# Computing the first 512 features behind each norm token tile by token tile, on a one-core transformer kernel

## The reference

```
h = rmsnorm(x, g);      x = x + short_conv_mixer(h)      # norm 0 before
x = x + conv_ffn(rmsnorm(x, g))                          # norm 1 before
x = x + moba_attention(rmsnorm(x, g))                    # norm 2 before
x = x + conv_ffn(rmsnorm(x, g));  x = rmsnorm(x, g)      # norm 3 before, norm 4 behind
x = layer_norm(ALPHA * x + even_mixer(x), g, b)          # norm 5
x = layer_norm(ALPHA * x + swiglu(x), g, b)              # norm 6
x = layer_norm(ALPHA * x + odd_mixer(x), g, b)           # norm 7
x = layer_norm(ALPHA * x + swiglu(x), g, b)              # norm 8, the output
```

## Time and profile before

| | us |
|---|---|
| median of 3 runs | 1309.02 (1308.71 to 1309.11) |
| the profiled execution | 1310.29 |
| its span, first to last instruction | 1309.0 |
| TensorE busy (matmul) | 1264.8 (97%) |
| VectorE busy | 815.9 (62%) |
| ScalarE busy | 616.7 (47%) |
| GpSimd busy | 68.7 (5%) |
| weights read | 211 MB in the span, 44% of the DMA engines' time |

### The profile page before, as it was taken

How to read it: one execution, slowest core, us unless ns; L and a number is a source line. 1 busy time by engine, 2 the same in 40 slices (tenths; PEclk the granted TensorE clock), 3 DMA queues, 4 the chain that set the end, 5 groups by cost and what they waited for, 6 DMA issues and landing times.

```text
span 1309.0 us, 20175 instructions
## 1 busy us (share of the span) xinstructions
PE 1264.8 (97%) x8548; PEld 1163.8 (89%) x8548; DVE 815.9 (62%) x1087; ACT 616.7 (47%) x775; POOL 68.7 (5%) x94
## 2 busy tenths in 40 slices
PE   7999999999998999999999999999998899999997
PEld 7999999887877999988998789999888887999986
DVE  6656777647665777763786675554467466655544
ACT  6445555434554555543674434443335653544430
POOL 0000000001000000000225200000001000000000
PEclk9999999999999999999999999999999999999999
DMA  9554454554431345554443345445434322644530
GB/s 356 213 194 154 185 194 172 213 190 182 161 129 65 145 181 176 192 194 176 169 161 131 132 186 190 172 184 199 169 121 161 130 97 97 225 173 182 193 129 32
DMA packets 32857, 219.37 MB, mean 168 GB/s; under 512 B 4224, under 2 KB 4480, under 8 KB 7680
## 3 DMA queue, kind: packets, MB, share of 16 engines
q1 hardware_dynamic: 30896, 211.27, 44.3%
q0 software_dynamic: 1872, 6.82, 1.5%
HBM read 217.01 MB, written 1.05 MB: 167 GB/s over the span
## 4 chain that ended last, share of the span: by engine, by line
PE 89%; DVE 6%; ACT 3%; issue 1%; POOL 1%; DMA 0%; DVEq 0%; ACTq 0%; POOLq 0%
PE ps L756 33%; PE ps L729 16%; PE ps L733 16%; PE ps L730 16%; PE ps L769 1%; DVE t L1272 1%; PE ps L791 1%; PE ps L818 1%; ACT t L991 1%; DVE t L1319 1%; POOL t L1634 1%; DMA t<-in_rows 0%; PE ps L803 0%; ACT t L1041 0%; PE ps L819 0%
## 5 line engine op out<-in xcount | busy, mean ns | idle before, releaser
L1272 DVE TENSOR_TENSOR t<-t,t 128x2048 fp32r<-128x2048 f32 (+2 forms) x201 | 454.9, 2268 | 173.5 <-PE ps L756 132.5
L756 PE MATMUL ps<-t,t 128*128 128x512 f32 (+2 forms) x2088 | 491.1, 392 | 12.3 <-DVE t L1341 3.6
L756 PEld LDWEIGHTS ps<-t,t 128*128 128x128 f32 x2088 | 384.5, 189 | 91.8 <-issue 9.5
L991 ACT CAST t<-t 128x2048 fp32r<-128x2048 f32 (+1 forms) x199 | 376.5, 1895 | 167.1 <-PE ps L756 151.3
L729 PE MATMUL ps<-t,t 128*128 128x256 f32 x1808 | 454.9, 284 | 0.2
L730 PE MATMUL ps<-t,t 128*128 128x256 f32 x1808 | 453.3, 283 | 0.0
L729 PEld LDWEIGHTS ps<-t,t 128*128 128x128 f32 x1808 | 347.0, 192 | 1.3 <-issue 1.0
L730 PEld LDWEIGHTS ps<-t,t 128*128 128x128 f32 x1808 | 347.0, 192 | 0.1
L733 PE MATMUL ps<-t,t 128*128 128x256 f32 x1808 | 290.6, 283 | 0.0
L733 PEld LDWEIGHTS ps<-t,t 128*128 128x128 f32 x1808 | 249.5, 192 | 0.0
L1329 DVE SCALAR_TENSOR_TENSOR t<-ps,t,t 128x255 f32<-128x255 f32 (+2 forms) x212 | 87.3, 476 | 51.3 <-ACT t L1006 42.1
(11 more groups left out here) (188 smaller groups left out, 743.9 us busy)
## 6 DMA issues: line engine op xcount, KB each, us to landing
t<-in_wts SPq DMA_DIRECT2D x196, 1024.0 KB, 4.8
t<-in_rows POOLq DMA_DIRECT2D x13, 512.0 KB, 4.6
t<-in_wts SPq DMA_DIRECT2D x2, 768.0 KB, 4.1
t<-in_x_in SPq DMA_DIRECT2D x2, 512.0 KB, 3.8
t<-in_wts SPq DMA_DIRECT2D x2, 512.0 KB, 3.6
out<-t SPq DMA_DIRECT2D x4, 256.0 KB, 2.0
t<-in_cst SPq DMA_DIRECT2D x1, 448.0 KB, 10.9
t<-in_pw SPq DMA_DIRECT2D x1, 256.0 KB, 5.8
```

The source lines that it names most:

```text
L756: ins = mm(ps[:, t_bank(stage, t, j), 0:c1 - c0], a, w[:, k, c0:c1], start=kt == 0 and part == 0, stop=kt == KTS[stage] - 1 and part == 2)
L991: copy(wh[:, k, 0:w], wraw[:, r, 0:w]).then_inc(s_hi, 1)
L1272: tt(wl[:, k, sl], wraw[:, r, sl], wh[:, h, sl].bitcast(F32), ALU.subtract).then_inc(s_lo, 1)
```

## The change

Behind norms 1 to 7 the first 512 features are computed as a **head**: in form T with one accumulator per token tile, tile 0 first. `head_steps` writes the order: all high passes of tile 0 (8 contraction tiles x 2 matmuls), then its low passes with the turning of tile 1's two halves among them, then tile 1. For the FFNs and the even mixer's u, the next stages want features by tokens; ScalarE copies each tile's result from PSUM to SBUF ("evict", into XN's tile 0) and TensorE turns it into banks 2 and 3 ("headturn"), from which what read chunks 0 and 1 now reads. q0 and cq are used as they lie. The head of an FFN holds 256 gate and 256 up features; its weights are packed as two chunks of four contraction tiles.

The warming matmuls behind the norms go (those at the program's start stay). At a layer norm the centring is a step of its own, and tile 0's two "rest" steps lie between tile 1's centrings and scalings. In an FFN the convolutions, silu and product of chunks 0 and 1 come after chunk 2, together with chunk 2's. In the even mixer the order becomes: u (the head), dt, x parts; dtsoft stands behind xconv0, and "ends" behind the second x chunk. In the odd mixer the fourth pump of the head stands before lrms0, where it stood behind it.

```diff
     def ffn(q, up_g, up_u, g0, u0, down, layer):
-        for m in range(11):
+        head(f"ffn{q}", (up_g, up_u), layer, [(g0, 256), (u0, 256)])
+        for m in range(1, 11):
...
+    head("even", ("even_w_in_2",), 0, [(0, 512)])
     f("even", "even_w_in_2", 0, 3072, 16, 128)
-    for m in range(2):
-        f("even", "even_w_in_2", 0, 256 * m)
...
-@q0 t0.0 t1.0 t2.0 t3.0 t4.0 t5.0 flush + t6.0 t7.0 t0.1 t1.1 t2.1 t3.1 t4.1 t5.1 t6.1 t7.1 + +
+@q0 head
...
-f0.0 dtcopy + f1.0 dtin f1.1 us0 + dtsoft f2.0 sum0 f2.1 us1 +
-f3.0 f3.1 xconv0 + xsilu0 mix0 f4.0 f4.1 sum1 xconv1 + xsilu1 ends f5.0 f5.1 xconv2 + xsilu2
-mix1 f6.0 f6.1 sum2 xconv3 + xsilu3 btok cb f7.0 mix2 f7.1 sum3 xconv4 + xsilu4 spread0
-f8.0 f8.1 xconv5 + xsilu5 mix3
+@even head f0.0 headturn dtcopy us0 us1 + f1.0 dtin sum0 f1.1 xconv0 + dtsoft xsilu0 sum1
+f2.0 mix0 f2.1 xconv1 + xsilu1 ends f3.0 mix1 f3.1 sum2 xconv2 + xsilu2 f4.0 f4.1 sum3 xconv3 + xsilu3 mix2
+f5.0 btok cb f5.1 xconv4 + xsilu4 spread0 mix3 f6.0 f6.1 xconv5 + xsilu5
...
-@cq t0.0 t0.1 t1.0 t1.1 t2.0 t2.1 t3.0 t3.1 + t4.0 t4.1 t5.0 t5.1 t6.0 t6.1 t7.0 t7.1 lrms0 +
+@cq head lrms0
...
-    elif b < 5:
-        out += [("warm", b, 6, WARM_RMS[0]), ("rest", b, 0, 0), ("stats", b, 1), ("rest", b, 0, 1),
-                ("norm", b, 1, 0), ("turn", b, 1, 0), ("warm", b, 7, WARM_RMS[1]), ("norm", b, 1, 1),
-                ("turn", b, 1, 1), ("rest", b, 1, 0), ("rest", b, 1, 1)]
-    else:
-        out += [("warm", b, 6, WARM_LN[0]), ("stats", b, 1), ("norm", b, 1, 0), ("turn", b, 1, 0),
-                ("warm", b, 7, WARM_LN[1]), ("norm", b, 1, 1), ("turn", b, 1, 1),
-                ("rest", b, 0, 0), ("rest", b, 1, 0), ("rest", b, 0, 1), ("rest", b, 1, 1)]
-    return out + [("pump",)] * (1 if lazy else 2)
...
+    if b < 5:
+        return out + [("rest", b, 0, 0), ("stats", b, 1), ("rest", b, 0, 1), ("norm", b, 1, 0), ("norm", b, 1, 1)]
+    return out + [("stats", b, 1), ("centre", b, 1, 0), ("rest", b, 0, 0), ("norm", b, 1, 0), ("rest", b, 0, 1),
+                  ("centre", b, 1, 1), ("norm", b, 1, 1)]
...
+def head_steps(h, b):
+
+
+    stage = f"head_{h}" if h in HEADED else h
+    lo = [("lo", stage, kt, 0) for kt in range(8)]
+    n = 4 if b >= 5 else 0
+    out = [("hi", stage, kt, 0) for kt in range(8)] + lo[:n] + [("turn", b, 1, 0)]
+    n, m = n, (8 if b >= 5 else 2)
+    out += lo[n:m] + [("turn", b, 1, 1)] + lo[m:]
+    if h in HEADED:
+        out.append(("evict", h, 0))
+    out += [("rest", b, 1, 0), ("rest", b, 1, 1), ("pump",), ("pump",)]
+    out += [("t", stage, kt, 1) for kt in range(4)] + [("pump",)]
+    if h in HEADED:
+        out.append(("headturn", h, 0))
+    out += [("t", stage, kt, 1) for kt in range(4, 8)]
+    if h in HEADED:
+        out.append(("evict", h, 1))
+    return out + [("pump",)]
+
+
+def ffn_steps(q, b):
+    out = head_steps(f"ffn{q}", b - 1)
+    for n in range(2, 22):
+        out += [("f", f"ffn{q}", n, 0)] + [("headturn", f"ffn{q}", 1)] * (n == 2) + [("f", f"ffn{q}", n, 1)]
+        done = (0, 1, 2) if n == 2 else (n,)
+        for m in done:
+            name = "product" if m % 2 else "silu"
+            out += [("conv", q, m)] * (q < 2) + [("pump",)] * (m == n) + [(name, q, m // 2)]
...
+        def head_turned(stage, t):
+            pe.wait_ge(*head_copied(stage, t))
+            for i in range(4):
+                if i % 2 == 0:
+                    pe.wait_ge(*acc_free(f_ready(stage), 1, i // 2))
+                ins = turn(head_bank(t, i), head_rows(t)[:, tok(i)], ident)
+            ins.then_inc(s_headt, 1)
...
+            elif kind == "evict":
+                stage, t = k
+                act.wait_ge(s_t, T_AT[("lo", f"head_{stage}", 7, 0) if t == 0 else ("t", f"head_{stage}", 7, 1)])
+                act.wait_ge(s_turn, xh_at(f_ready(stage), 0, t))
+                copy(head_rows(t), ps[:, t, :]).then_inc(s_headc, 1)
```

More of the change, by code:

```diff
@@ L31, in t, with head @@
             plan.append((stage, "T", name, layer, [(c0, n)], n, per, k))
+    def head(stage, name, layer, cols):
+        for k in (0, 4):
+            plan.append((f"head_{stage}", "T", name, layer, cols, 512, 4, k))
     def ffn(q, up_g, up_u, g0, u0, down, layer):
-        for m in range(11):
+        head(f"ffn{q}", (up_g, up_u), layer, [(g0, 256), (u0, 256)])
+        for m in range(1, 11):
             f(f"ffn{q}", up_g, layer, g0 + 256 * m)
@@ L80, with f_chunk @@
 KTS = {stage: len(c) * PER[stage] for stage, c in CHUNKS.items()}
+HEADED = ("ffn0", "ffn1", "ffn2", "ffn3", "even")
+def f_chunk(stage, n):
+    return CHUNKS[stage][n - 2 if stage[:3] == "ffn" else n]
 VEC = {}
@@ L185, in mixed_steps @@
             steps.append(("pump",))
-        elif word == "flush":
-            steps += [("turn", 2, 1, 0), ("turn", 2, 1, 1), ("rest", 2, 1, 0), ("rest", 2, 1, 1)]
+        elif word == "head":
+            steps += head_steps(stage, b - 1)
+        elif word == "headturn":
+            steps.append(("headturn", stage, 1))
         elif word == "end":
@@ L227, in end_steps @@
-    return out + [("pump",)] * (1 if lazy else 2)
-def ffn_steps(q, b, lazy=False):
-    out = []
-    for n in range(22):
-        out += [("f", f"ffn{q}", n, 0), ("f", f"ffn{q}", n, 1)]
-        name = "product" if n % 2 else "silu"
-        out += [("conv", q, n), ("pump",), (name, q, n // 2)] if q < 2 else [(name, q, n // 2), ("pump",)]
+        return out + [("stats", b, 1)] + normed_steps(b, 1, 0) + normed_steps(b, 1, 1) + [("pump",)] * 2
+    if b < 5:
+        return out + [("rest", b, 0, 0), ("stats", b, 1), ("rest", b, 0, 1), ("norm", b, 1, 0), ("norm", b, 1, 1)]
@@ L254, in all_steps @@
     out += end_steps("sc_out", 1)
-    out += [("rows", 2)] + ffn_steps(0, 2, True)
+    out += [("rows", 2)] + ffn_steps(0, 2)
     out += [("rows", 3), ("zero_kv",)] + mixed_steps(MOBA, None, 3)
@@ L276, in releases @@
         _, stage, kt, t = s
-        return (kt % PER[stage] == PER[stage] - 1 and t == 1) or s == ("t", "q0", 7, 0)
+        return kt % PER[stage] == PER[stage] - 1 and t == 1
+    if s[0] == "lo":
+        return s[2] == 7
     if s[0] == "part":
@@ L735, in f_block, with t_part @@
                 ins.then_inc(s_f, 1)
-        def t_part(step, stage, kt, t, js):
+        def t_part(step, stage, kt, t, js, passes=(0, 1, 2)):
             per = PER[stage]
@@ L744, in t_part @@
             pe.wait_ge(s_lo, split_at(i))
-            if stage == "q0":
-                pe.wait_ge(s_xh, xh_at(2, t, kt // 4))
+            one_tile = stage[:4] == "head" or stage in ("q0", "cq")
+            if one_tile:
+                pe.wait_ge(s_xh, xh_at(t_norm(stage), t, kt // 4))
             else:
                 pe.wait_ge(*t_ready(stage, kt))
-            for part, (a, w) in enumerate(((hi, H), (hi, L), (lo, H))):
-                if stage == "q0" and part == 2:
-                    pe.wait_ge(s_xl, xl_at(2, t, kt // 4))
+            for part in passes:
+                a, w = ((hi, H), (hi, L), (lo, H))[part]
+                if one_tile and part == 2:
+                    pe.wait_ge(s_xl, xl_at(t_norm(stage), t, kt // 4))
                 for j in js:
@@ L770, in turn_rows @@
             ins.then_inc(s_turn, 1)
-        def warm(b, bank, n):
-            pe.wait_ge(s_mask, 1)
-            for _ in range(n):
-                pe.wait_ge(*turn_bank_free(b, bank))
-                mm(ps[:, bank, 0:256], identr[:], maskr[:], start=True, stop=True)
+        def head_turned(stage, t):
[5 more added lines that the diff above has]
+            ins.then_inc(s_headt, 1)
         def scores(a, h):
@@ L1313, in normed @@
                 return
-            mean, sq = (st[:, 16 * t + i:16 * t + i + 1] for i in (12, 13))
-            dve.settle()
-            dve.own(stt(out=xs, in0=rs, scalar=mean, in1=grow[:, sl], op0=ALU.subtract, op1=ALU.mult))
+            sq = st[:, 16 * t + 13:16 * t + 14]
             dve.settle()
```

94 lines of the change are left out of this document (61 added, 33 removed).

## The result

| | before | after |
|---|---|---|
| median, same chip | 1308.87 (1307.91 to 1309.11) | 1294.05 (1293.20 to 1294.28) |
| ratio | | 0.9887, 95% interval 0.9870 to 0.9904 |
| the profiled execution's span | 1309.0 | 1293.0 |
| TensorE busy, matmuls | 1264.8, 8548 | 1248.6, 8186 |

The change saves 14.8 us by the medians and 16.0 by the two profiled spans (the profiled execution of the kernel before took 1310.29, 1.4 us over its median here); the forecast was 20 (1289.0, range 1284.0 to 1293.5), so the time lies 0.5 us above the range.

The account below looks back on a forecast made before the run. At norms TensorE waits for a chain in which VectorE is busiest, its warming computing nothing; 6.7 + 0.9 + 8.9 + 0 + 3.4 = 19.9 us off 1309.0 gives 1289, range 1284 to 1293.5.

Parts of the forecast that it names:

- Norms 1, 2, 3, 5 and 7: Heads keep TensorE fed: RMS norms 1 and 3 gain 6.7 us together, norm 2 0.9, layer norms 5 and 7 8.9.
- The three paces: TensorE matmul times: 0.229 us with tokens stationary, 512 columns; 0.120 with weights stationary, 256 columns; 0.109 per turn.
- the 0.1 us of spare at the layer norms: Tile 1's second half ready at T + 5.85, last turn group starting at T + 5.95, so the wait is covered.
- The evictions: Two ScalarE copies per head, 0.59 us each, delay weight casts and splits but stay hidden behind TensorE's work.
- the FFN's backlog: Chunks 0 to 2 reach ScalarE and VectorE together; chunk 6 waits at T + 35.8, convolution ends about T + 26: no cost.
- rival C: FFN heads stall because the first chunks' backlog holds banks 4 to 7; four heads give nothing: 1304.7 us, chance 0.04.
- Norm 4: Even mixer: head gains 3.35 us, a 3.6 stall at "ends" eats it; +0.75 or -0.8 with clock, taken as 0.
- the hole before 992.27: TensorE gap of 3.5 us in the odd mixer before, followed by about 3.2 us at half clock, 1.6 lost.
- Rival B: Mixers pay more: the stall at "ends" reaches 6 to 8 us, delaying the last convolution; 1292 to 1294, chance 0.12.
- Norm 6: Odd mixer: head ends 5.65 us earlier, late ukv weight delays squares; gain 3.4, clock falls in either order and cancels.
- Rival D: Without warming TensorE falls to 1.2 GHz in each head; decides from 45 us, 5.7 lost per norm; 1378, chance 0.03.
- The drain: Skill's 1.38 us on top of 1.28 per table switch; by it decay logs in the even mixer come 4.1 later.

Follow-up runs that it names:

- e1: Changed kernel with the softplus of dt moved ahead of the first convolution in the even mixer: 1286.08 us, ratio 0.9816 to the kernel before.
- e3: Changed kernel with 33 matmuls that nobody reads ahead of the "ends" matmuls in the even mixer: 1290.63 us, ratio 0.9844 to the kernel before.
- e5: The changed kernel run again without an edit: 1294.18 us, ratio 0.9867 to the kernel before.
- e6: Changed kernel with the odd mixer's fourth pump back behind cq's squares and two weight-split pumps moved behind the latents: 1289.07 us, ratio 0.9831 to the kernel before.
- e10: Changed kernel with 40 matmuls that nobody reads ahead of the uq matmuls in the odd mixer: 1290.69 us, ratio 0.9841 to the kernel before.
- e2: Changed kernel with the "ends" matmuls moved behind the third x chunk, softplus left in place: 1287.72 us, ratio 0.9829 to the kernel before.
- e9: Changed kernel with 16 matmuls that nobody reads ahead of the "ends" matmuls in the even mixer: 1291.63 us, ratio 0.9848 to the kernel before.
- e11: Changed kernel with tile 0's low parts at layer norms put behind both centrings and scalings of tile 1: 1301.32 us, ratio 0.9918 to the kernel before.
- e7: Kernel before with only the warming matmuls behind its norms taken out: 1320.98 us, ratio 1.0078 to the kernel before.

## Why the prediction was right where it was, and wrong in the sum

*Norms 1, 2, 3, 5 and 7: right.* 16.5 forecast (6.7 + 0.9 + 8.9), and 17.6 came (8.6 + 4.5 + 4.5 by the marks). The 1 us too little is spread over the first three: from T to T, norm 1 gave 3.6, norm 2 1.3 and norm 3 3.6, and 0.2 was gained ahead of norm 1, where nothing was changed. The three paces, the closed stream of 12.8 us and the 0.1 us of spare at the layer norms held, but for 0.10 us of idle time at norm 6 (956.77 to 956.87), where the count had 0.1 to spare.

*The evictions and the FFN's backlog: right.* No idle time of TensorE behind the evictions, and none at a sixth chunk; rival C is out.

*Norm 4: the step that failed.* The stall at "ends" was sized well: 3.6 forecast, 3.9 measured, ready at T + 31.8 against 31.2. Two terms behind it failed. First, the text had the last convolution follow ScalarE's and VectorE's own list, at 684.75, so that 0.75 of the gain would be left; e1 and the changed kernel show that it follows TensorE's stream, 3.8 to 3.9 us behind it in both, so the whole stall goes through: 3.35 less 3.9 is -0.5, not +0.75. Second, I named the clock's price behind the hole, took it from the hole before 992.27 (3.5 us, 1.6 lost), and then left it out of the value that I took ("I take 0"). It was 2.7 to 2.8 (e3), and the stage repeats: 144.0, 144.4 and 144.4 us in e5, e6 and e10, which leave it unedited. Together -3.3 of the -3.8; the other 0.5 isn't accounted for. Rival B named the first of these mechanisms but tied it to a stall of 6 to 8 us; it needed none so long.

*Norm 6: half right.* The landing of the weight, the squares behind the cast and the start of uq came as worked out (gain 3.5, forecast 3.4). The step "the clock falls after this hole in either order, which cancels" failed: the clock behind it cost 1.5 us in the profiled execution of the kernel before and 2.8 in that of the changed one (e10). That is the 1.25 us between 3.4 and 2.2. The hole also grew, from 3.5 to 4.84 us, since TensorE reached it earlier by more than VectorE did, but that this made the price isn't shown: the same hole cost 1.4 to 1.9 in e2, e3, e9 and e11. By the 142.4 to 142.8 us of e2, e3 and e9 this stage would have gained 4.6 to 5.0, more than forecast. So 2.2 is the gain of one execution, and the cause of the difference stays open.

*The sum.* 3.8 too much at norm 4 and 1.2 at norm 6, about 1 too little elsewhere: 3.9, and with the rounding of 1289.1 to 1289.0 the distance to the span's 1293.0. The forecast's own range was also added up too narrowly: with norm 4 at -1.5, norm 6 at 2 and 0.3 per head lost, the gain is 14.9 and the slow end 1294.1, not 1293.

*Rival D* put a hole at each of seven norms at 11 us in all; six of them in the kernel before cost 10 (e7), so that term was well sized. Its next one isn't: 45 us at 1.2 GHz lose some 22 us, or 3.2 per norm, not 5.7.

*The drain.* The Trainium skill (ScalarE: Activation LUTs, "What ACT_TABLE_LOAD costs") has each switch of tables cost 2.7 us with its drain. The trace after disagrees as the one before did: load at 644.84, 1.28 long, activation at 646.13. Rival B's stall of 6 to 8 us by that figure didn't come.

## What to carry to other kernels

Price a hole on the busiest engine as two terms, its length and the clock behind it, and take the second into the value, not only into the range; a clock term on both sides of an edit need not cancel, since one and the same hole cost 1.4 to 2.8 us here. Judge an edit by the stage that it changes: the odd mixer moved by almost 3 us between profiles without an edit in it. When work is moved forward on the bounding engine, list for each in-order queue which small producer it now overtakes, and move that producer (a softplus here, and 6.9 us by it) rather than fill the gap. A step ahead of a transfer that has not landed holds everything queued behind it: 4.1 us of ScalarE here, for squares that had long been ready to start.
